# Hybrid decoder step: first projection columns loaded by halves of features, second half of the modulation spread between single feature blocks

## The reference

```python
mod = silu(c) @ w_ada + b_ada
shift, scale, gate = split(mod, 3)
h = x * (1 + scale) + shift
z = h @ w_in                        # 2976 columns, split into nine parts
# MLA attention (8 heads) from cq, ckv, kr; gated linear attention (4 heads) from gq, gk, gv, glr
mla = mla_o * silu(g_mla);  gla = rms_norm(gla_o) * silu(g_gla)
x = layer_norm(alpha * x + gate * (concat(mla, gla) @ w_out))
```

## Time and profile before

| | |
|---|---|
| median of 3 runs | 774.85 us (773.21 to 775.33) |
| the profiled execution's own time | 775.36 us |
| its span, first to last instruction | 773.6 us |
| PE busy | 724.0 us (94%) |
| DVE, ACT, POOL busy | 346.8, 327.9, 75.5 us |
| mean granted clock of PE | 0.987 |

### The profile page before, as it was taken

The page is one execution under the profiler, slowest core; times in us unless marked ns, Lnnn a source line. Parts: engine busy times, 40 slices in busy tenths (PEclk is TensorE's granted clock), DMA queues, the critical chain, the costliest instruction groups (busy, mean ns, idle before and its releaser), DMA issues.

```text
span 773.6 us, 16831 instructions
## 1 busy us (share of the span) xinstructions
PE 724.0 (94%) x7073; PEld 553.9 (72%) x7073; DVE 346.8 (45%) x769; ACT 327.9 (42%) x783; POOL 75.5 (10%) x113
## 2 busy tenths in 40 slices
PE   2689999999999999999989899999999989999996
PEld 1467777877779996777765577777668878668884
DVE  0424342020101024687675756675661111377967
ACT  1315381021112135767544655566665656701100
POOL 0000000000000010101121122002112442000000
PEclk9799999999999999999999999999999999999999
DMA  9957030300301001000010200021215997102332
GB/s 297 397 223 269 1 109 1 108 1 3 90 1 55 1 28 55 16 8 16 9 11 1 55 2 1 1 55 61 78 69 183 317 366 252 58 14 87 120 136 82
DMA packets 35287, 70.33 MB, mean 91 GB/s; under 512 B 6611, under 2 KB 17964, under 8 KB 33549
## 3 DMA queue, kind: packets, MB, share of 16 engines
q1 hardware_dynamic: 30586, 47.73, 18.8%
q0 software_dynamic: 4016, 20.97, 7.4%
q10 hardware_dynamic: 610, 0.55, 0.3%
HBM read 62.26 MB, written 6.07 MB: 88 GB/s over the span
## 4 chain that ended last, share of the span: by engine, by line
PE 88%; DVE 4%; DMA 3%; SPq 2%; ACT 2%; issue 1%; POOL 0%; DVEq 0%; ACTq 0%; POOLq 0%
PE banks L1956 26%; PE banks L2140 8%; PE banks L2269 4%; PE banks L2350 4%; PE banks L2371 3%; PE banks L1965 3%; PE banks L2109 3%; PE banks L2500 2%; PE banks L2502 2%; PE banks L2501 2%; PE banks L2046 2%; PE banks L2440 2%; PE banks L2459 2%; PE banks L2483 2%; DMA s_x<-in_x_prompt 2%; PE banks L2484 1%
## 5 line engine op out<-in xcount | busy, mean ns | idle before, releaser
L1006 ACT ACTIVATE s_z<-banks 128x512 f32<-128x512 f32 (+3 forms) x48 | 24.4, 517 | 157.2 <-PE banks L1956 157.2
L1956 PE MATMUL banks<-s_w_parts,s_h_b 128*128 128x512 f32 (+3 forms) x360 | 81.1, 330 | 1.2 <-DVE s_h_b L1381 1.2
L1956 PE MATMUL banks<-s_z_r,s_h_b 128*128 128x512 f32 (+1 forms) x216 | 69.8, 390 | 0.0
L1216 ACT ACTIVATE s_z<-banks 128x512 f32<-128x512 f32 (+1 forms) x88 | 41.3, 517 | 52.2 <-PE banks L2350 52.0
L1956 PE MATMUL banks<-s_w_parts,s_h_a 128*128 128x512 f32 (+2 forms) x288 | 62.3, 322 | 0.0
L1956 PEld LDWEIGHTS banks<-s_w_parts,s_h_b 128*128 128x128 f32 x360 | 55.2, 189 | 8.7 <-issue 1.7
L1956 PE MATMUL banks<-s_z_r,s_h_a 128*128 128x512 f32 x192 | 61.4, 396 | 0.0
L1421 DVE COPY s_front<-banks 128x512 f32<-128x512 f32 (+2 forms) x5 | 2.9, 589 | 125.8 <-PE banks L1921 125.8
L1207 ACT ACTIVATE s_z<-banks,s_temps 128x128 f32<-128x128 f32 (+7 forms) x64 | 47.1, 741 | 4.4 <-DVE s_temps L1684 3.7
L1956 PEld LDWEIGHTS banks<-s_z_r,s_h_b 128*128 128x128 f32 x216 | 40.5, 188 | 10.4 <-ACT s_z L1006 1.7
L1956 PEld LDWEIGHTS banks<-s_w_parts,s_h_a 128*128 128x128 f32 x288 | 42.0, 189 | 4.8 <-issue 0.4
(11 more groups left out here) (384 smaller groups left out, 1414.0 us busy)
## 6 DMA issues: line engine op xcount, KB each, us to landing
s_z<-in_w_ada SPq DMA_DIRECT2D x16, 512.0 KB, 12.0
s_temps<-in_w_in SPq DMA_DIRECT2D x3, 2048.0 KB, 8.2
s_x<-in_x_prompt SPq DMA_DIRECT2D x8, 512.0 KB, 11.7
s_z<-in_w_ada SPq DMA_DIRECT2D x1, 4096.0 KB, 12.7
s_kt<-in_w_out SPq DMA_DIRECT2D x8, 512.0 KB
s_temps<-in_x_prompt SPq DMA_DIRECT2D x8, 512.0 KB
out_y_prompt<-s_temps SPq DMA_DIRECT2D x7, 512.0 KB
s_temps<-in_w_in SPq DMA_DIRECT2D x1, 1664.0 KB, 16.8
```

The source lines that it names most:

```text
L1006: nc.scalar.activation(z[:, t, CHUNKS[c][0]:CHUNKS[c][1]], banks[:, proj_bank(c, t), 0:WIDTH[c]], ACT.Silu if c in (1, 3) else ACT.Copy).t ...
L1216: nc.scalar.activation(PTb[r % 3][:, 4 * g:4 * g + n, :], banks[:, 4 + (groups(r) + g) % 2, 0:P * n].rearrange("p (j q) -> p j q", j=n), A ...
L1956: last = nc.tensor.matmul(banks[:, proj_bank(c, t), 0:WIDTH[c]], h_[half][:, k, n0:n0 + P], w_, start=(k == 0 and n == 0), stop=(k == KT - ...
```

## The change

It has three parts. First, the first chunk of `w_in` comes in two transfers, each of four feature blocks (832 KB): the first where the whole was, the second after the modulation's second half. ACT splits each half by an instruction of its own, and DVE's `low_first(4)` and `low_first(7)` move behind it. Second, PE's order: pieces of the modulation stand before or between whole feature blocks, `first_rows(3)` stands after the turn, and some transposes move forward. Third, the transposed block k = 6 of the first half goes to bank 6, which is free once the modulation's second half has been carried out, and waits move to match. SP's wait for the gate columns now also asks for the second half of the first columns.

```diff
@@ x_bank, w_parts_ready
-            return 4 + k % 2 if half == 0 else 4 + k % 4
+            return (6 if k == 6 else 4 + k % 2) if half == 0 else 4 + k % 4
-            return (k + 1 if k < 5 else min(KT, k + 2)) if c == 0 else KT + 2 * (c - 1) + k // 4 + 1
+            return (k + 1 if k < 5 else {7: 6, 5: 7, 6: 8}[k]) if c == 0 else KT + 2 * (c - 1) + k // 4 + 1
@@ SP
+            def first_columns_in(half):
+                part = slice(4 * half, 4 * half + 4)
+                sp.dma_start(w_raw[0][:, part, :], w_in[:, part, CHUNKS[0][0]:CHUNKS[0][1]]).then_inc(rest_in if half else w_in_in[0], 16)
             for kk in range(KT // 2):
                 ada_columns(0, kk)
-            columns_in(0)
+            first_columns_in(0)
             rows_in(0)
             for kk in range(KT // 2):
                 ada_columns(1, kk)
+            first_columns_in(1)
             rows_in(1)
+            sp.wait_ge(rest_in, 16)
             sp.wait_ge(modT_done, 2)
-            sp.dma_start(ada_gate, w_ada[:, :, 2 * D:3 * D]).then_inc(gate_in, 16)
+            sp.dma_start(ada_gate, w_ada[:, :, 2 * D:3 * D]).then_inc(rest_in, 16)
@@ ACT
-            split_w(0)
+            def split_first(half):
+                act.wait_ge(rest_in if half else w_in_in[0], 16)
+                part = slice(4 * half, 4 * half + 4)
+                nc.scalar.activation(w_hi[0][:, part, :], w_raw[0][:, part, :], ACT.Copy).then_inc(w_hi_ready, 1)
+
+            split_first(0)
...
             for k in range(1, 4):
                 high(0, k)
+            split_first(1)
             act.wait_ge(modT_ready, 8)
@@ DVE
-            for k in (0, 1, 2, 3, 4, 7):
+            for k in range(4):
                 low_first(k)
             bring(0, 0)
             low(0, 0)
             bring(0, 3)
             for k in range(1, 4):
                 low(0, k)
+            low_first(4)
+            low_first(7)
             modulation(1)
-            low(0, 4)
             modulation_samples(1)
             low_first(5)
+            low(0, 4)
+            bring(0, 6)
             low(0, 5)
-            bring(0, 6)
@@ PE, rows_transposed
-                if half == 0 and k >= 2:
+                if half == 0 and k == 6:
+                    pe.wait_ge(mod_ready, 4)
+                elif half == 0 and k >= 2:
                     brought(pe, 0, k - 2)
                 if half == 1:
-                    if k < 2:
-                        brought(pe, 0, k + 6)
+                    if k == 0:
+                        brought(pe, 0, 4)
+                    if k == 1:
+                        brought(pe, 0, 7)
@@ PE, order (first_rows now always takes all four row tiles)
             for k in range(4):
                 rows_transposed(0, k)
-            first_rows(0, all_four)
             modulation(1, 0)
-            first_rows(1, all_four)
-            modulation(1, 1)
+            first_rows(0)
             rows_transposed(0, 4)
             rows_transposed(0, 5)
-            first_rows(2, all_four)
+            modulation(1, 1)
             modulation(1, 2)
-            first_rows(3, range(2))
+            first_rows(1)
             modulation(1, 3)
-            first_rows(3, range(2, 4))
+            first_rows(2)
             modulation_turned(1)
             rows_transposed(0, 6)
-            first_rows(4, all_four)
+            first_rows(3)
             rows_transposed(0, 7)
-            first_rows(5, all_four)
-            samples_part(0)
+            first_rows(4)
             pe.wait_ge(x_in[1], 64)
             rows_transposed(1, 0)
-            first_rows(6, all_four)
+            first_rows(5)
+            brought(pe, 0, 6)
+            samples_part(0)
             rows_transposed(1, 1)
-            first_rows(7, all_four)
-            for k in range(2, KT):
+            first_rows(6)
+            rows_transposed(1, 2)
+            rows_transposed(1, 3)
+            first_rows(7)
+            for k in range(4, KT):
                 rows_transposed(1, k)
```

More of the change, by code:

```diff
@@ L409, in hybrid_step @@
         ada_in = [sem(f"ada_in{i}") for i in range(KT)]
-        gate_in = sem("gate_in")
+        rest_in = sem("rest_in")
         gate_used = sem("gate_used")
@@ L1900, in gate_columns @@
             def gate_columns():
-                pe.wait_ge(gate_in, 16)
+                pe.wait_ge(rest_in, 32)
                 brought(pe, 1, 7)
@@ L1958, in rows_projected, with first_rows @@
                 last.then_inc(proj_done, 1)
-            def first_rows(k, tiles):
+            def first_rows(k):
                 pe.wait_ge(w_ready, w_parts_ready(0, k))
                 pe.wait_ge(h_ready, k + 1)
-                for t in tiles:
+                for t in range(4):
                     for n, (h_, w_) in enumerate(((h_hi, w_hi[0][:, k, :]), (h_hi, w_lo_first[k]), (h_lo, w_hi[0][:, k, :]))):
@@ L2142, in head_scores @@
                 last.then_inc(sc_done, 1)
-            first_half, all_four = range(2), range(4)
             for kk in range(4):
```

## The result

The changed kernel took 764.21 us (median of 4 runs, 762.08 to 767.19) against 774.03 for the kernel before (4 runs, 772.0 to 775.33): ratio 0.9878, 95% interval 0.9837 to 0.9919. The sign was right. Two later comparisons, on different chips, gave 0.9886 (0.9853 to 0.9919) and 0.9939 (0.9911 to 0.9967). Over all 22 executions of the changed kernel the mean is 765.5, over 91 of the kernel before 772.0: a gain of 6.5 us with a 95% interval of about 1.2 either way. (Seven executions of all kernels that are on record as slow, over 1.5% above the fastest of their kernel, are left out of the means and intervals here.) So the first result shows 3.3 us more gain than the pooled executions, and that is about what the forecast gain was off by (3.2).

A forecast was written before the change was run, and what follows sets the result against it. PE was taken as the bound, through its waits and slow clock. Gains 2.1 (x) + 0.2 - 0.1 (first wait, clock) + 2.5 (idle) + 1.8 (clock) = 6.5, taken as 6.6 from 774.85, gave 768.2 us; range 765.0 to 771.3.

The forecast's parts named there:

- Part 1, x's landing: Ahead of x: with half of the first columns moved behind, x is complete at 25.2 instead of 27.3, gaining 2.1 us.
- The hand-over: From turn to split block 4: idle falls from 3.02 to 0.5 us, gaining 2.5, and the clock should not fall.
- What reaches the turn: PE's own work through block 2 ends at 43.3 us and the modulation's turn follows then.
- rival C: Second half of the columns lands late and delays the turn; in full 773.1 us, range 770.3 to 773.5; chance 0.13.
- no idle over 0.6 us between 29 and 60: Sign on PE's timeline: no idle span longer than 0.6 us from 29 to 60 us.
- rival B: Before x, PE's clock may stay at 2.4 GHz: 2 to 4 us more gain, 764 to 766 us; chance 0.10.
- are done at 40.7 at the latest: On DVE, the two low parts ahead of the modulation's carrying out finish by 40.7 us, before it starts at 41.0.
- The sum: Front, up to the second half's rows: gains total 6.5 us, start at 64.0 instead of 70.48; 6.6 taken.
- the clock's term: PE's front: block 4 after the hand-over costs 2.29 us, not 4.06, gaining 1.8; 0.1 lost in the first slow stretch.
- lower clock about even: First slow stretch after x: 4.2 us of multiplications at half clock, to 33.4, costing about as before; 0.1 us lost.
- The idle's term: PE's idle from x to the second half's rows: 2.5 us saved at the hand-over and 0.2 at the first wait.
- My forward count: Block times added forward from block 2's end at 43.3: second half's rows start at 62.8, a gain of 7.7 us.

The follow-up runs named there:

- the eight others: Profiles of six edited kernels: part 1 alone; parts 2 and 3 alone; low parts later (twice); late half last; PE kept busy; block 3 before the turn (twice); 764.80 to 773.37 us.

## Why the prediction was right or wrong

**Part 1, x's landing: right.** 2.1 predicted, 1.86 measured (27.30 to 25.44), DVE just in time as computed (26.30 against 26.4). The queue with the halves in it moved 387 to 393 GB/s, as before. The Trainium skill (DMA: Bandwidth & Descriptors, "Bandwidth") says to batch transfers to at least 1 MiB for 75% of the peak; a loss from halves of 832 KB does not show here, where the transfers queue behind one another.

**The hand-over: right.** Idle behind the turn 0.26 (I had 0.5) instead of 2.82, between 0.23 and 0.26 in all three profiles, and no slow stretch behind it in any. The relay from turn to block 4 took 4.06 us (4.13).

**What reaches the turn: right in time, wrong in cause.** I had 43.3 and measured 42.8, but I had PE's own work end there. It was rival C in a mild form: the late half landed at 38.7, later than my 37.0 to 38.1; DVE was free at 41.3 instead of 39.6 to 40.7, and PE had run out of work at 41.3. One of my signs, no idle over 0.6 us between 29 and 60, failed with the 1.45 us there. And it was rival B too: the first slow stretch ended at 29.35, not 33.4. The two cancelled. My statement that the low parts "are done at 40.7 at the latest" and cost nothing is the one that failed; the runs with that order turned round and with the half issued last show that the half sets the turn. As a consequence the clock before the turn, which I priced at half of its stretch, is worth nothing in the changed kernel as long as it is slow for 6.8 us or less.

**The sum: mis-sized.** "2.1 + 0.2 - 0.1 + 2.5 + 1.8 = 6.5". By the same terms the first pair of traces gives: x 1.9; idle from x to the second half's rows 4.42 before (0.22, 0.20, 1.40, 1.42, 1.18) and 3.06 after (0.19, 1.45, 0.26, 1.16), so 1.4 instead of 2.7; busy time at half clock 11.8 before and 3.2 after, so 4.3 instead of 1.7; 0.4 in smaller gaps. Together 8.0. So the clock's term was too small by 2.6, and the part of it that failed is the first slow stretch, for which I took "lower clock about even" (0.1 lost): PE was busy for 8.3 us at half clock there before and for 3.2 after, worth 2.6. The idle's term was too large by 1.3, for the 1.45 us before the turn. The second profile of the kernel before, with a slow stretch 3.4 us shorter, takes 2.2 off: 5.8. So the front is worth 5.8 to 8.0, and 6.6 lay inside. My forward count (62.8) was nearer to the start at 62.5 than the sum (64.0), in part by luck: it had block 4 start at 47.4 instead of 46.85 and the work from there on at 15.4 us instead of 15.64. (My first paragraph speaks of five idle spans and lists six.)

Over all executions the clock's share looks smaller. The mean granted clock is 0.9892 in the 22 executions of the changed kernel and 0.9873 in 87 of the kernel before (its first four have none on record), which makes 16.5 and 19.5 us at half clock: 3.1 less, with an interval of 2.9 either way. Half of that is 1.5 us, by this estimate near the 1.7 of my sum and far from the 4.3 of the first pair.

**The range: this is why the time lay outside.** It was built from the front alone, and set at 774.85, a median of three. Where nothing was changed the executions differ by more than my range was wide. From 13 profiles of eight kernels:

```
                       before, before again   changed, again, third   the eight others
second half's rows at  70.5, 68.3             62.5, 62.2, 62.6        60.4 to 68.6
to the gather loop     519.7, 520.1           520.6, 525.3, 522.1     519.4 to 526.5
  of it at half clock  3.4, 3.4               3.4, 13.7, 10.2         0 to 17.1
gather loop            57.3, 54.6             53.5, 56.0, 52.6        52.5 to 56.8
rest                   126.0, 126.0           126.0, 126.0, 126.0     126.0 to 126.1
```

The middle stretch follows its slow clock; the gather loop varies by up to 4.8 us by itself. Together they take 574.1 to 581.3 us in the three profiles of the changed kernel, 7 apart. In those three PE was busy for 51.3 to 51.4 us of the loop and idle for 2.2, 4.6 and 1.2, mostly until gathered keys had landed, so what lengthens the loop there is PE's waiting. The longest loop, of the first profile of the kernel before, had 4.1 us of idle and 53.2 of busy time.

Pooled medians are 764.9 for the changed kernel and 772.0 for the one before, 7.1 apart. So of the 4.0 us between 768.2 and 764.2, 2.9 are the level (774.85 was that much too high), 0.5 the gain, and 0.6 the luck of four short executions. The range failed narrowly: the changed kernel's pooled median of 764.9 lies just below its end at 765.0, its pooled mean of 765.5 inside. The profile I started from was itself a slow one (the longest first slow stretch and the longest gather loop seen).

**What stays open.** Whether the slow stretches at 305, 391 and 445 us come by chance alone or more often with the changed kernel's timing: the slow clock of the middle stretch was 3.4 us in both profiles of the kernel before and 3.4, 13.7, 10.2 in the changed one, and three are too few. The clocks of all executions lean the same way: the profiled fronts have 5.7 us at half clock on average in the changed kernel and 11.9 in the one before, some 6 less, but the whole executions only 3.1 less. With an interval of 2.9 that isn't shown. What made PE's busy time in the first profile's gather loop 2 us longer is open too, and so is how much of the difference between 0.9886 and 0.9939 belongs to the chips.

## What to carry to other kernels

When a load is split and its second half goes behind other transfers, look at what stands behind its consumer on each engine: here two small low parts on DVE stood ahead of a step that the whole kernel waited for, and the half's landing became the new bound. Give an engine that hands over to two others a block of work to do meanwhile: it saves idle and, in those executions where the clock would have fallen, the slow restart as well. And before a gain of 1% is forecast from one profile, take a second one of the same kernel: the stretches that the change doesn't touch differed by 7 us between three profiles of the changed kernel, as much as the whole gain. And when two profiles are compared for one part of a change, compare those with equally long slow stretches.

## What the hardware showed beside that

- PE's clock fell after the same idle (1.63 and 0.68 us at the hand-over) in one execution and not in another, and slow stretches lasted 3.4, 6.8 or 10.2 us; in the changed kernel's first profile it rose at 29.35, when PE had run x's transposes from 25.44 to 29.06 (0.19 us of it idle) and a piece of the modulation for 0.3, while in the earlier trace rows it stayed down through such transposes and 4.4 us of multiplications. The first slow stretch of the kernel before lasted 10.2 us in one profile and 6.8 in the other, and the second half's rows started 2.2 us apart: a saving priced from one slow stretch is no better than that.
- A landing's time varies far less than PE's clock: with the columns in halves PE began x's transposes at 25.0 to 25.5 in nine profiles, and ACT took up the late half at 38.45 to 39.24 in nine, while the first slow stretch lasted 0 to 6.8 us.
